# Attention's probabilities normalised inside the product that turns them, dense fillers ahead of waits, and a first retention pass in another order

## The chip, the cores and the metric

## The reference, cut to what matters

The program is a two-layer model (gated delta rule, mLSTM, and their MLPs) followed by a third layer that mixes retention and attention. The change touches waits around mLSTM and around the third layer's context norm, and the two mixers of the third layer:

```
def _dense_attention(q, k, v):                 # 8 query heads, 2 key heads, 512 queries, 768 keys
    s = jnp.einsum('bqkgd,bskd->bkgqs', q, k).astype(jnp.float32) * ATT_SCALE
    p = jax.nn.softmax(s, axis=-1).astype(v.dtype)
    return jnp.einsum('bkgqs,bskd->bqkgd', p, v)

# retention, per head, both directions; chunked in the reference
scores = jnp.einsum('bhid,bhjd->bhij', qf, kf) * intra      # intra: decay by distance
o = (jnp.einsum('bhij,bhjv->bhiv', scores, vf)
     + jnp.einsum('bhid,bhdv->bhiv', qf, state) * q_dec)

# mLSTM ends in a norm over each head, the context in one over its rows
hs = rms_norm(hs, w_norm.reshape(MLSTM_HEADS, MLSTM_DV)) * jax.nn.sigmoid(o...)
hc = _modulate(_rmsnorm(xc, norm1_g), csh1, csc1)
```

All is float32, 512 tokens plus 16 meta tokens.

## The kernel before, in words

Five engines run hand-ordered instruction streams that meet only in semaphores: `S("name")` is a count that one engine adds to and another waits for. There is no scheduler; the order of the code is the order of each engine. Most of the time is PE's: weights are split into a high and a low part (ACT L322 copies the high part, DVE L329 subtracts for the low part), and every product is three matmuls (L306).

**Attention** (`pe_att`, `act_att`, `dve_att`) works in 32 units of 128 queries of one head against 768 keys. For unit n, PE computes the scores into PSUM (L2775, 128x384 twice), DVE takes the row maximum (L2888) and negates it (L2891), ACT computes the exponentials into `a_p` with their row sum (L2827), DVE takes the inverse of the sum (L2895) and multiplies `a_p` (128x768) by it (L2897), PE turns the six 128x128 tiles of `a_p` (L2783), and ACT copies the turned tiles to SBUF (L2848). PE's order per unit is: scores of unit n+2, turning of unit n, and, in three of eight units, a third of the product with the values of the head pair before (L2793). DVE's order is: maximum of unit n+1, then inverse and scaling of unit n. The turned tiles have one place in PSUM (banks 4 and 5), so the turning of unit n waits for the copy of unit n-1. Among the first units stand the norm sums and factors of retention (L2658, L2677, L2711), which share PE and DVE.

**Retention** (`pe_ret`, `act_ret`, `dve_ret`, `pool_ret`) works in two passes of two heads. In each, DVE computes the exponents of the decay table `r_tt` (L2574, L2576) and the decayed context keys (L2582, L2583), ACT the exponentials for the queries (L2553) and the table (L2556), then copies the turned values `r_vT` (L2559); PE waits for `r_vT` and the context keys before the state product (L2633), and for DVE's decayed scores before the next scores (L2607). ACT's and DVE's passes are loops with registers for the pass. Ahead of the first pass ACT splits a block of weights (L322).

**Norms and waits.** `pe_norm` sums squares by a product with ones (L357), and after the inverse root comes back spreads it over rows (L366). It is called for the context (turn 5) between two blocks of the third layer's input product. `pe_mls_gates` turns the gates of mLSTM (L1853, L1854) once DVE has done its part (L1843). At the end of mLSTM PE sums squares of the last chunk in two halves (L1869), turns the statistics (L1937), and spreads the factors of the 8 heads (L1944), from which DVE forms the input of the output product tile by tile (L2101, L2105).

Of the kernel before, what the change touches and what calls it, by code (L numbers as in the profile page):

```python
# [14 lines left out]
P = 128  # L15
# [104 lines left out]
def build_program(nc, A, out):  # L120
    with ExitStack() as ctx:
# [248 lines left out]
        def pe_norm(pe, turn, pieces, sq=n_sq, to=6):  # L370

            pe_norm_sums(pe, turn, pieces, sq, bank=4)
            pe_norm_rows(pe, turn, pieces, to)
# [1475 lines left out]
        def pe_mls_gates(pe):  # L1849
            pe.wait_ge(S("gates_a"), GDN_A + 9)  # L1850
# [331 lines left out]
        a_pT = [at(f"a_pT{y}", [P, KEYS // P, SEQ], SB_G + 4 * 2 * T * 2 + RH * SEQ * 4 + y * KEYS // P * SEQ * 4) for y in range(2)]  # L2182
        a_pT2 = aa_r.take("a_pT2", [P, KEYS // P, SEQ])
# [172 lines left out]
        def pe_b2_in(pe):  # L2356
# [12 lines left out]
            pe_norm(pe, 5, CTXP, sq=ctx_sq, to=5)  # L2369
# [177 lines left out]
        def act_ret(act):  # L2547
            act.sem_inc(S("r_out"), 2)
            with act.Fori(0, RH // 2) as i:
                for x in range(2):  # L2550
                    act.wait_ge(S("r_o"), i * 2 + (x + 1))
                    for d in range(2):
                        act.activation(r_qd[x][d][:, :], b_pos[:, d, :], ACT.Exp, scale=b_lg[:, bass.ds(i * 2 + (RH * d + x), 1)])\  # L2553
                            .then_inc(S("r_qe"), 1)
                    act.wait_ge(S("r_t"), i * 2 + (x + 1))
                    act.activation(r_tt[x][:, :], r_tt[x][:, :], ACT.Exp).then_inc(S("r_te"), 1)  # L2556
                for x in range(2):
                    act.wait_ge(S("v_turned"), i * 2 + (MLS_HALVES + x + 1))
                    act.activation(r_vT[x][:, :, :], ps[:, 4 * x, :].rearrange("p (a t) -> p a t", a=4), ACT.Copy).then_inc(S("v_copied"), 1)  # L2559
                for x in range(2):  # L2560
                    act.wait_ge(S("r_sd"), i * 2 + (x + 1))
                    act.activation(r_S[x][:, :, :], ps[:, 4 * x, 0:2 * P].rearrange("p (a t) -> p a t", a=2), ACT.Copy).then_inc(S("r_S"), 1)
                for x in range(2):
                    fixed_wait(act)
                    act.wait_ge(S("r_o"), i * 2 + (x + 3))
                    act.activation(b_q[:, bass.ds(i * 2 + x, 1), :].rearrange("p a t -> p (a t)"), ps[:, 4 * x + 1, :], ACT.Copy)\
                        .then_inc(S("r_out"), 1)

        def dve_ret(dve):
            with dve.Fori(0, RH // 2) as i:  # L2570
                for x in range(2):
                    lg = [b_lg[:, bass.ds(i * 2 + (RH * d + x), 1)] for d in range(2)]
# [193 lines left out]
        def pe_att(pe):  # L2766
# [463 lines left out]
```

## Time and profile before

| what | value |
|---|---|
| median of 3 runs | 2556.2 us |
| the profiled execution's own time | 2550.86 us |
| its span, first to last instruction | 2549.0 us |
| PE busy | 2453.0 us (96%) |
| DVE, ACT, POOL busy | 56%, 33%, 10% |
| mean granted PE clock | 0.978 |
| the chain that ended last | PE 87%, DVE 7%, ACT 3%, issue 2% |

The chain is followed back from the last instruction to what released it each time; an engine's share in it is time that sets the end. The profiled execution lasted 5.3 us less than the median. Spans are counted from the first instruction.

### The profile page before, as it was taken

How to read it: one execution, taken by the hardware profiler on the slowest of the kernel's cores; microseconds unless marked ns; L12 is line 12 of the kernel's file. 1: busy time of each engine (PE TensorE's matmuls, PEld its weight loads, DVE VectorE, ACT ScalarE, POOL GpSimd, SP SyncE). 2: the span in 40 equal slices, each digit the busy share in tenths (PEclk: the TensorE clock that was granted, in tenths of full speed). 3: DMA queues.
4: the chain of work that ended last, by engine and by line, in shares of the span. 5: the costliest groups of instructions: out<-in, count | busy, mean ns of one | idle time of the engine just before them, and what ended most of it. 6: DMA issues, size and time to landing. Idle time of an engine off the chain costs nothing.

```text
span 2549.0 us, 41060 instructions
## 1 busy us (share of the span) xinstructions
PE 2453.0 (96%) x17237; PEld 2229.6 (87%) x17237; DVE 1415.8 (56%) x1954; ACT 837.5 (33%) x1196; POOL 261.3 (10%) x203
## 2 busy tenths in 40 slices
PE   7999999999999999999998999999999899999998
PEld 7999999998999999999987788888997446998996
DVE  5677656654553443543566666667466464544443
ACT  5433444444321221322323322224323353322332
POOL 2000222323100000100021000002012101000001
PEclk9999999989999999999998999999999899999999
DMA  3222533335222222222101444543311001222221
GB/s 137 83 84 72 129 84 90 87 60 196 83 84 100 83 92 89 94 89 83 66 1 70 154 156 165 182 155 140 108 58 43 17 1 50 83 86 96 99 83 66
DMA packets 93885, 235.70 MB, mean 92 GB/s; under 512 B 60074, under 2 KB 61700, under 8 KB 69556
## 3 DMA queue, kind: packets, MB, share of 16 engines
q1 hardware_dynamic: 88208, 201.40, 23.8%
q10 hardware_dynamic: 5540, 32.30, 3.5%
q8 instruction: 107, 1.75, 0.3%
q14 instruction: 30, 0.25, 0.0%
HBM read 222.00 MB, written 11.67 MB: 92 GB/s over the span
## 4 chain that ended last, share of the span: by engine, by line
PE 87%; DVE 7%; ACT 3%; issue 2%; DMA 1%; POOL 0%; ACTq 0%; DVEq 0%; POOLq 0%; SPq 0%
PE ps L306 68%; PE ps L1128 1%; PE ps L1142 1%; PE ps L2775 1%; PE ps L1118 1%; PE ps L310 1%; PE ps L2793 1%; PE ps L2783 1%; DVE c_DA L2028 1%; PE ps L1154 1%; PE ps L1155 1%; ACT whi L322 1%; PE ps L1160 1%; DVE g_tmp L1342 1%; PE ps L1076 1%
## 5 line engine op out<-in xcount | busy, mean ns | idle before, releaser
L306 PE MATMUL ps<-xa_hi,whi 128*128 128x264 f32 (+2 forms) x2944 | 654.2, 296 | 24.3 <-DVE wlo L329 13.1
L306 PE MATMUL ps<-xa_lo,whi 128*128 128x264 f32 (+2 forms) x2944 | 649.8, 295 | 0.0
L306 PE MATMUL ps<-xa_hi,wlo 128*128 128x264 f32 (+2 forms) x2944 | 649.2, 295 | 0.0
L306 PEld LDWEIGHTS ps<-xa_hi,whi 128*128 128x128 f32 x2944 | 468.7, 190 | 42.1 <-DVE wlo L329 15.1
L322 ACT ACTIVATE whi<-raw 128x2048 fp32r<-128x2048 f32 x161 | 307.4, 1909 | 559.0 <-PE ps L306 546.7
L306 PEld LDWEIGHTS ps<-xa_lo,whi 128*128 128x128 f32 x2944 | 467.8, 190 | 11.1
L306 PEld LDWEIGHTS ps<-xa_hi,wlo 128*128 128x128 f32 x2944 | 467.3, 190 | 10.8
L329 DVE TENSOR_TENSOR wlo<-raw,whi 128x2048 fp32r<-128x2048 f32 x161 | 369.5, 2295 | 189.0 <-ACT whi L322 186.3
L306 PE MATMUL ps<-xb_lo,whi 128*128 128x264 f32 (+1 forms) x1280 | 384.4, 341 | 0.0
L306 PE MATMUL ps<-xb_hi,whi 128*128 128x264 f32 (+1 forms) x1280 | 382.5, 339 | 1.8 <-DVEq L248 1.5
L306 PE MATMUL ps<-xb_hi,wlo 128*128 128x264 f32 (+1 forms) x1280 | 382.6, 340 | 0.0
L306 PEld LDWEIGHTS ps<-xb_hi,whi 128*128 128x128 f32 x1280 | 220.2, 188 | 32.5 <-ACTq L248 2.4
L306 PEld LDWEIGHTS ps<-xb_lo,whi 128*128 128x128 f32 x1280 | 219.7, 188 | 27.9
L306 PEld LDWEIGHTS ps<-xb_hi,wlo 128*128 128x128 f32 x1280 | 220.0, 189 | 27.3
L381 POOL TENSOR_TENSOR n_sq<-n_sq 128x512 f32<-128x512 f32 (+1 forms) x42 | 76.0, 1810 | 1252.4 <-ACT n_sq L391 1250.3
L690 DVE TENSOR_TENSOR h<-ps,h 128x528 f32<-128x528 f32 (+1 forms) x88 | 61.2, 697 | 176.6 <-PE ps L306 175.4
L620 ACT ACTIVATE xb_hi<-m_y 128x528 fp32r<-128x528 f32 (+1 forms) x64 | 40.9, 639 | 280.0 <-DVE m_y L667 280.0
L692 DVE SCALAR_TENSOR_TENSOR h<-ps,b_mod,h 128x512 f32<-128x512 f32 x40 | 30.0, 749 | 113.1 <-PE ps L306 113.1
L865 DVE SCALAR_TENSOR_TENSOR conv_acc<-conv_in,par,conv_acc 128x528 f32<-128x528 f32 x96 | 73.8, 769 | 7.3 <-DVE conv_acc L862 0.2
L664 DVE SCALAR_TENSOR_TENSOR m_act<-ps,rstd 128x528 f32<-128x528 f32 (+1 forms) x64 | 44.5, 695 | 50.5 <-PE ps L306 48.7
L670 DVE TENSOR_TENSOR xb_lo<-m_y,xb_hi 128x528 fp32r<-128x528 f32 (+1 forms) x64 | 44.8, 700 | 45.1 <-ACT xb_hi L620 45.1
L614 ACT ACTIVATE m_y<-m_act 128x512 f32<-128x512 f32 x32 | 23.2, 724 | 115.9 <-DVE m_act L652 115.9
(423 smaller groups left out, 2820.4 us busy)
## 6 DMA issues: line engine op xcount, KB each, us to landing
raw<-weights SPq DMA_DIRECT2D x161, 1024.0 KB, 4.8
mod_w<-weights_mod ACTq DMA_DIRECT2D x24, 1024.0 KB, 4.7
g_EC<-scr_g SPq DMA_DIRECT2D x10, 424.0 KB, 5.2
scr_z<-z_st SPq DMA_DIRECT2D x16, 264.0 KB, 4.6
g_D<-scr_g SPq DMA_DIRECT2D x10, 371.0 KB, 5.2
scr_a<-g_AT SPq DMA_DIRECT2D x10, 318.0 KB
h<-x_in ACTq DMA_DIRECT2D x4, 528.0 KB, 9.5
z_b<-scr_z SPq DMA_DIRECT2D x1, 2112.0 KB
```

Of the source, the lines that this page charges most:

```text
L306: mm = pe.matmul(ps[:, at_ + step * c + bank, 0:tn], w[:, hb.slot, k, c * P:(c + 1) * P], x[:, k, t0:t0 + tn], start=(k == 0 and n == 0), ...
L310: mm = pe.matmul(ps[:, 6 + c, 0:en], w[:, hb.slot, k, c * P:(c + 1) * P], (elo if n == 1 else ehi)[:, k, 0:en], start=(k == 0 and n == 0), ...
L322: act.activation(whi[:, hb.slot], raw[:, hb.raw_slot], ACT.Copy).then_inc(S("w_hi"), 1)
L329: dve.tensor_tensor(wlo[:, hb.slot], raw[:, hb.raw_slot], whi[:, hb.slot].bitcast(F32), ALU.subtract).then_inc(S("w_lo"), 1)
L381: pool.tensor_tensor(flat(sq[:, 0], pieces), flat(sq[:, 0], pieces), flat(sq[:, k], pieces), ALU.add)\
L620: act.activation(flat(xb_hi[:, t], pieces), flat(m_y[:, c], pieces), ACT.Copy).then_inc(S("two_hi"), 1)
L664: dve.scalar_tensor_tensor(cols(m_act[:, c], pieces), pair(c, pieces), 0.0, cols(rstd, pieces), ALU.max, ALU.mult)\
L670: dve.tensor_tensor(flat(xb_lo[:, t], pieces), flat(m_y[:, c], pieces), flat(xb_hi[:, t], pieces).bitcast(F32), ALU.subtract).then_inc(S(" ...
L690: ins = dve.tensor_tensor(x, pair(c, pieces), x, ALU.add)
L692: ins = dve.scalar_tensor_tensor(x, pair(c, pieces), scale(2 * j + c), x, ALU.mult, ALU.add)
L865: ins = dve.scalar_tensor_tensor(conv_acc[:, c, :], x, w, conv_acc[:, c, :], ALU.mult, ALU.add)
L1076: mm = pe.matmul(ps[0:CH, 4 * x + 3, q * P:(q + 1) * P], qkv[:, 8 + 2 * g + q // 2, c], g_S[:, 4 * g + q, :], start=True, stop=True)
```

## The change: what it does

Four edits.

1. In attention, DVE no longer scales the 128x768 probabilities. It scales the 128x128 identity to a diagonal `a_dg` of the inverse sums, and PE multiplies each tile of `a_p` with it, where it turned the tile with `transpose` before.
2. A new helper `pe_keep` issues n float32 matmuls of ones with ones (128x128) into a bank whose contents are dead. 12 go between the context norm's sums and rows, 14 ahead of the gates' wait, 6 and 11 ahead of the two waits of mLSTM's last sums, 5 and 5 ahead of the two waits behind them. A wait for `c_kw` guards the bank.
3. ACT's and DVE's passes over retention are written out without registers. In the first pass ACT copies the turned values before the exponentials, and DVE forms the context keys before the table's exponents. The second pass keeps its order.
4. ACT's split of weights moves from ahead of the first retention pass to behind its state copies.

```diff
+        def pe_keep(pe, n, bank):
+            for _ in range(n):
+                pe.matmul(ps[:, bank, 0:P], ones[:, :], ones[:, :], start=True, stop=True)
...
             pe_norm_sums(pe, turn, pieces, sq, bank=4)
+            pe_keep(pe, keep, to)
             pe_norm_rows(pe, turn, pieces, to)
...
         def pe_mls_gates(pe):
+            pe_keep(pe, 14, 4)
             pe.wait_ge(S("gates_a"), GDN_A + 9)
...
-            def sums(i):
+            def sums(i, keep=(0, 0)):
                 for x in range(2):
+                    pe_keep(pe, keep[x], 1)
                     pe.wait_ge(S("c_sq"), i * 2 + x + 1)
...
-            sums(NCH - 1).then_inc(S("head_sums"), 8)
+            pe.wait_ge(S("c_kw"), 2 * NCH)
+            sums(NCH - 1, (6, 11)).then_inc(S("head_sums"), 8)
 
         def pe_mls_rows(pe):
+            pe_keep(pe, 5, 1)
             pe.wait_ge(S("head_inv"), 6)
...
+            pe_keep(pe, 5, 1)
             pe.wait_ge(S("head_lo"), 3)
...
+        a_dg = [aa_r.take(f"a_dg{c}", [P, P]) for c in range(2)]
...
-            pe_norm(pe, 5, CTXP, sq=ctx_sq, to=5)
+            pe_norm(pe, 5, CTXP, sq=ctx_sq, to=5, keep=12)
...
         def act_ret(act):
...
+            for i in range(RH // 2):
+                for part in (values, decays) if i == 0 else (decays, values):
+                    part(i)
...
+                if i == 0:
+                    act_split(act, HalfBlock(HB_B2_OUT + 1))
...
         def dve_ret(dve):
...
+            for i in range(RH // 2):
+                for part in (context, tables) if i == 0 else (tables, context):
+                    part(i)
...
-                    mm = pe.transpose(ps[:, 4 + t // 3, (t % 3) * P:(t % 3 + 1) * P], a_p[n % 2][:, t * P:(t + 1) * P], ident[:, :])
+                    mm = pe.matmul(ps[:, 4 + t // 3, (t % 3) * P:(t % 3 + 1) * P], a_p[n % 2][:, t * P:(t + 1) * P], a_dg[n % 2][:, :],
+                                   start=True, stop=True)
...
-                    dve.tensor_scalar(a_p[c][:, :], a_p[c][:, :], a_inv[c][:, 0:1], None, ALU.mult).then_inc(S("at_n"), 1)
+                    dve.tensor_scalar(a_dg[c][:, :], ident[:, :], a_inv[c][:, 0:1], None, ALU.mult).then_inc(S("at_n"), 1)
...
-                lambda: (act_split(act, HalfBlock(HB_B2_OUT + 1)), act_ret(act)),
+                lambda: act_ret(act),
```

The order on ACT at the first retention pass, before: `whi` is the weight split, `r_qd` and `r_tt` the exponentials, `r_vT` the turned values, `r_S` the states. The loop begins at L2549, and `r_vT` stands behind its four `r_qd` and two `r_tt`.

```order
L2477 ACTIVATE b_dec<-b_dec 128x16
L322 ACTIVATE whi<-raw 128x2048
L2549 UNCONDITIONAL_BRANCH
L2549 ISA
L2553 ISA
L2553 ACTIVATE r_qd_178<-b_pos,b_lg 128x512
```

And in the change, the same place on ACT:

```order
L2489 ACTIVATE b_dec<-b_dec 128x16
L2574 ACTIVATE r_vT_187<-ps 128x512
L2574 ACTIVATE r_vT_188<-ps 128x512
L2567 ACTIVATE r_qd_178<-b_pos,b_lg 128x512
L2567 ACTIVATE r_qd_179<-b_pos,b_lg 128x512
L2569 ACTIVATE r_tt_185<-r_tt_185 128x896
L2567 ACTIVATE r_qd_180<-b_pos,b_lg 128x512
L2567 ACTIVATE r_qd_181<-b_pos,b_lg 128x512
L2569 ACTIVATE r_tt_186<-r_tt_186 128x896
L2581 ACTIVATE r_S_193<-ps 128x256
L2581 ACTIVATE r_S_194<-ps 128x256
L322 ACTIVATE whi<-raw 128x2048
```

The two value copies now come first, and the split last of the group.

The end of mLSTM on PE before: `c_sq` are the squares, `head_stat` the statistics, `mh_hi` and `mh_lo` the factors.

```order
L1921 MATMUL ps<-c_W_133,c_VA_137 128x106
L1869 MATMUL ps<-ones,c_sq 106x64 x8
L1937 MATMUL ps<-ident,head_stat 8x106 x5
L1944 MATMUL ps<-mh_hi,head_one 128x512
L1944 MATMUL ps<-mh_lo,head_one 128x512
```

And in the change, with the fillers (L373):

```order
L1929 MATMUL ps<-c_W_133,c_VA_137 128x106
L373 MATMUL ps<-ones 128x128 x6
L1877 MATMUL ps<-ones,c_sq 106x64 x4
L373 MATMUL ps<-ones 128x128 x11
L1877 MATMUL ps<-ones,c_sq 106x64 x4
L373 MATMUL ps<-ones 128x128 x5
L1947 MATMUL ps<-ident,head_stat 8x106 x5
L373 MATMUL ps<-ones 128x128 x5
L1955 MATMUL ps<-mh_hi,head_one 128x512
```

27 fillers stand between products that stood next to each other.

The beginning of attention on PE before: `a_kd` and `a_qst` are the scores, `ident` and `a_p` the turning, `rn_sq` retention's norm sums.

```order
L2775 MATMUL ps<-a_kd,a_qst_206 128x384 x2
L2783 MATMUL ps<-ident,a_p_214 128x128 x6
L2775 MATMUL ps<-a_kd,a_qst_207 128x384 x2
L2783 MATMUL ps<-ident,a_p_213 128x128 x6
L2677 MATMUL ps<-ones,rn_sq 128x64 x16
```

And in the change:

```order
L2801 MATMUL ps<-a_kd,a_qst_206 128x384 x2
L2809 MATMUL ps<-a_dg_226,a_p_214 128x128 x6
L2801 MATMUL ps<-a_kd,a_qst_207 128x384 x2
L2809 MATMUL ps<-a_dg_225,a_p_213 128x128 x6
L2703 MATMUL ps<-ones,rn_sq 128x64 x16
```

Nothing moves here; the moving operand of the six products is now the diagonal. These rows count a float32 product once, where the trace shows two matmuls for it: the scores stand as x2 a unit here and as x128 over 32 units in the trace.

## Rows read from the trace of the kernel before

**Rows 1.** The page: busy time, share, instructions.
```profile
PE 2453.0 (96%) x17237; PEld 2229.6 (87%) x17237; DVE 1415.8 (56%) x1954; ACT 837.5 (33%) x1196; POOL 261.3 (10%) x203
```
**Rows 2.** Windows: stretch, length, busy of PE, PEld, DVE, ACT, POOL, PEclk, DMA.
```profile
1175.80:1179.20 3.40, 3.40 (x16) 3.36 (x16) 0.58 (x2) 0.00 (x0) 0.00 (x0) 0.50 0.85 294
1346.40:1363.40 17.00, 13.18 (x37) 9.64 (x38) 10.21 (x18) 7.79 (x14) 1.98 (x1) 0.50 0.00 1
1783.40:1790.10 6.70, 3.08 (x14) 3.08 (x15) 4.27 (x8) 1.50 (x4) 0.00 (x0) 0.50 0.40 126
1954.00:1957.30 3.30, 3.30 (x16) 3.30 (x17) 2.17 (x4) 0.53 (x2) 2.14 (x2) 0.50 0.02 5
2022.40:2035.80 13.40, 11.16 (x27) 6.17 (x28) 7.04 (x15) 5.58 (x9) 0.00 (x0) 0.50 0.00 0
2059.90:2063.20 3.30, 3.30 (x11) 2.24 (x10) 2.33 (x8) 1.49 (x4) 0.00 (x0) 0.50 0.02 5
2111.10:2117.80 6.70, 4.72 (x17) 2.22 (x17) 0.78 (x2) 1.83 (x4) 0.00 (x0) 0.50 0.01 2
```
**Rows 3.** Chain of waits, the context norm: start, length, piece.
```profile
1787.02 1.22 PE ps L366 x4
```
**Rows 4.** Chain of waits, the end of mLSTM.
```profile
1347.42 1.71 PE ps L1869 x8
...
1349.91 1.06 PE ps L1937 x5
...
1352.96 7.19 PE ps L1944 x16
```
**Rows 5.** Timeline, DVE, end of mLSTM's output tiles: start, length, instruction.
```profile
1354.29 1.47 DVE L2101 TENSOR_TENSOR mh_y<-ml,ps 128x512 f32<-128x512 f32 x2 [1.39 <-PE ps L1944]
...
1364.51 1.63 DVE L2105 SCALAR_TENSOR_TENSOR xb_lo<-mh_y,par,xb_hi 128x512 fp32r<-128x512 f32 x2
```
**Rows 6.** Chain of waits, retention: state product and what follows, both passes.
```profile
1953.92 3.65 PE ps L2633 x16
1957.58 3.43 PE ps L2607 x8
...
1977.55 1.78 PE ps L2633 x16
```
**Rows 7.** Timeline, retention's first pass on ACT and DVE.
```profile
1947.15 1.91 ACT L322 ACTIVATE whi<-raw 128x2048 fp32r<-128x2048 f32 x1 [0.27 <-issue]
...
1951.14 0.75 DVE L2582 TENSOR_TENSOR r_ck<-ps,b_dec 128x256 f32<-128x256 f32 x2
...
1953.10 1.06 ACT L2559 ACTIVATE r_vT<-ps 128x512 f32<-128x512 f32 x2
...
1953.70 2.47 DVE L2591 TENSOR_TENSOR r_w<-ps,r_tt 128x512 f32<-128x512 f32 x4
```
**Rows 8.** Attention by form, 1994 to 2122: count, busy us, mean ns, idle before.
```profile
L2783 PE MATMUL ps<-ident,a_p 128*128 128x128 f32 x192 | 30.4, 300 | 16.5 <-DVE a_p L2897 15.5 <-ACT a_pT L2848 1.0
...
L2897 DVE TENSOR_SCALAR a_p<-a_p,a_inv 128x768 f32<-128x768 f32 x32 | 20.5, 639 | 1.1
...
L2891 DVE TENSOR_SCALAR a_nm<-a_mx 128x1 f32<-128x1 f32 x32 | 4.9, 154 | 1.1
```
**Rows 9.** DVE's lines by form, the whole span: the nearest tensor_scalar.
```profile
L455 DVE TENSOR_SCALAR n_y<-n_y,b_modc 128x256 f32<-128x256 f32 x8 | 2.8, 354 | 0.3
```
**Rows 10.** Chain of waits, 1994.3 to 2123.3: shares by line, then three pieces.
```profile
by line: PE ps L2775 22.9%; PE ps L2793 18.2%; PE ps L2783 16.9%; DVE a_mx L2888 8.1%; DVE a_p L2897 5.9%; issue 4.1%; PE ps L2711 2.8%; PE ps L2677 2.7%; PE ps L2658 2.7%; ACT a_p L2827 2.3%; DVE xb_lo L2860 2.1%; ACT xb_hi L2832 1.6%; DVE
...
2045.36 1.87 PE ps L2793 x8
2047.23 1.49 PE ps L2775 x4
2048.72 0.66 PE ps L2783 x6
```
**Rows 11.** Line L2783: what PE's idle time ahead of it ended with.
```profile
  DVE a_p L2897: 44.3, 32
```

More of the change, by code:

```diff
@@ L368, in pe_norm_rows, with pe_norm @@
             mm.then_inc(S("norm_all"), 1)
-        def pe_norm(pe, turn, pieces, sq=n_sq, to=6):
+        def pe_keep(pe, n, bank):
+            for _ in range(n):
+                pe.matmul(ps[:, bank, 0:P], ones[:, :], ones[:, :], start=True, stop=True)
+        def pe_norm(pe, turn, pieces, sq=n_sq, to=6, keep=0):
             pe_norm_sums(pe, turn, pieces, sq, bank=4)
+            pe_keep(pe, keep, to)
             pe_norm_rows(pe, turn, pieces, to)
@@ L2548, in act_ret, with decays @@
             act.sem_inc(S("r_out"), 2)
-            with act.Fori(0, RH // 2) as i:
+            def decays(i):
                 for x in range(2):
@@ L2552, in act_ret, with values @@
                     for d in range(2):
-                        act.activation(r_qd[x][d][:, :], b_pos[:, d, :], ACT.Exp, scale=b_lg[:, bass.ds(i * 2 + (RH * d + x), 1)])\
-                            .then_inc(S("r_qe"), 1)
+                        n = RH * d + 2 * i + x
+                        act.activation(r_qd[x][d][:, :], b_pos[:, d, :], ACT.Exp, scale=b_lg[:, n:n + 1]).then_inc(S("r_qe"), 1)
                     act.wait_ge(S("r_t"), i * 2 + (x + 1))
                     act.activation(r_tt[x][:, :], r_tt[x][:, :], ACT.Exp).then_inc(S("r_te"), 1)
+            def values(i):
                 for x in range(2):
@@ L2562, in act_ret, with tables @@
                     act.activation(r_S[x][:, :, :], ps[:, 4 * x, 0:2 * P].rearrange("p (a t) -> p a t", a=2), ACT.Copy).then_inc(S("r_S"), 1)
+                if i == 0:
+                    act_split(act, HalfBlock(HB_B2_OUT + 1))
                 for x in range(2):
-                    fixed_wait(act)
                     act.wait_ge(S("r_o"), i * 2 + (x + 3))
-                    act.activation(b_q[:, bass.ds(i * 2 + x, 1), :].rearrange("p a t -> p (a t)"), ps[:, 4 * x + 1, :], ACT.Copy)\
-                        .then_inc(S("r_out"), 1)
+                    act.activation(b_q[:, 2 * i + x, :], ps[:, 4 * x + 1, :], ACT.Copy).then_inc(S("r_out"), 1)
         def dve_ret(dve):
-            with dve.Fori(0, RH // 2) as i:
+            def tables(i):
                 for x in range(2):
-                    lg = [b_lg[:, bass.ds(i * 2 + (RH * d + x), 1)] for d in range(2)]
+                    lg = [b_lg[:, RH * d + 2 * i + x:RH * d + 2 * i + x + 1] for d in range(2)]
                     dve.wait_ge(S("r_o"), i * 2 + (x + 1))
@@ L2576, in dve_ret, with context @@
                     dve.scalar_tensor_tensor(r_tt[x][:, :], b_tau[:, 1, :], lg[1], r_tt[x][:, :], ALU.mult, ALU.add).then_inc(S("r_t"), 1)
+            def context(i):
                 for x in range(2):
@@ L2580, in dve_ret @@
                     for d in range(2):
-                        w = b_dec[:, d, bass.ds(i * 2 + x, 1), :].rearrange("p a l -> p (a l)")[:, :, None].to_broadcast([P, 2, P])
+                        w = b_dec[:, d, 2 * i + x, :][:, :, None].to_broadcast([P, 2, P])
                         dve.tensor_tensor(r_ck[x][:, d], c[:, 0], w, ALU.mult)
                     dve.tensor_copy(r_cv[x][:, :, :], c[:, 1]).then_inc(S("r_c"), 1)
+            for i in range(RH // 2):
+                for part in (context, tables) if i == 0 else (tables, context):
+                    part(i)
+                for x in range(2):
                     dve.wait_ge(S("r_te"), i * 2 + (x + 1))
```

## The prediction

> **What bounds the kernel now.** I read the page's busy times first, then the granted clock, then the chain of waits at each place that the change touches. PE is busy 96% of the span [rows 1], so a saving counts only where PE waits, or where its clock is at the lower level. The windows show where it is: seven stretches at 0.50, that is 1.2 GHz, all behind a place where PE stood idle or did little [rows 2]. In such a stretch PE's work takes twice its time. The first four lie where fillers or the retention edit go, the last three in attention. In attention PE's idle time ahead of the turning, 44.3 us over 32 units, ended with DVE's scaling [rows 11]. That looks like the bound, but the chain says otherwise: the scaling has 5.9% of 129.0 us, 7.6 us, the turning itself 16.9%, 21.8 us, and scores and value products 41% [rows 10]. Where a unit has a value product in front, PE goes from one to the next without waiting: 1.87, 1.49 and 0.66 us [rows 10].
>
> **The product with the diagonal.** A turned tile costs 0.66 / 6 = 0.11 us on PE at full clock [rows 10]. A 128x128 float32 product stands in the trace too: retention's state product has 8 of them, as 16 matmuls in 1.78 us, so 0.222 us each; at the lower clock the same took 3.65 us, 0.456 each [rows 6]. The turning is 192 matmuls for 192 tiles [rows 8], one each, where the product needs two. Six tiles so cost 1.33 in place of 0.66 us: +0.67 a unit, and twice that at 1.2 GHz. The ends are 0 (the product runs like the turning) and +2.1 (all at the lower clock: 6 x 0.456 - 0.66); I take +0.67, the row of the same shape.
>
> The Trainium skill speaks against this edit. "Perfetto Trace Analysis", section "Transposes", says that a logical transpose should be issued as a transpose and not as a standard matmul, since transposes skip the arithmetic; and "TensorE: Matmul & The Clock Gate", section "Terms", calls the transpose mode 4 times as fast for FP32. By that figure a tile would cost an estimated 0.44 us; the rows of this case say twice, not four times, and the measurement of the same shape decides for the sum.
>
> DVE's scaling takes 0.62 to 0.64 us for 768 columns, and 0.154 for one [rows 8]; for 256 it takes 0.354 [rows 9]. For 128 I take 0.25, between those last two, which are the ends. The saving is 0.38 us a unit (0.28 to 0.48).
>
> Which unit pays and which saves is read off the chain. The turning has 25 pieces in it, the scaling 12, one of these only 0.04 long. So +0.67 x 25 = +16.8 us and -0.38 x 11 = -4.2. Around 2084 to 2091 the chain runs over DVE alone and a unit lasts 2.0 to 2.4 us; with the product PE needs 1.29 + 1.33 = 2.62 for scores and product, so PE takes over there: +1.2 over three or four units. Against that stands the clock. The stretch at 2059.9 follows 2.1 us of idle PE; the longer products in front of it and the shorter scaling behind leave about 1 us, so I expect it to stay at full clock: 3.3 / 2 = -1.6. The last stretch, 6.7 us with 4.7 of work in it, goes the same way, for the three last turnings come closer together: -1.9 of a possible 2.4. The long one, 13.4 us, begins behind retention's square roots, where PE waits 4.6 us in any case; it falls again, but dense products may end it a step earlier: -1.0 net of what the product costs twice in it. Attention together: 16.8 - 4.2 + 1.2 - 1.6 - 1.9 - 1.0 = **+9.3 us**. If the clock gives nothing back it is +13.8.
>
> **The fillers.** Each is a 128x128 float32 product, 0.222 us at full clock, 0.456 at the lower [rows 6].
> - Gates: 14 make 3.1 us in an idle time of 4.6 that ends with DVE's part at 1175.3, so nothing is late. PE then worked 3.4 us at 0.50 [rows 2]; if the clock stays up, half goes: -1.7. If it falls all the same, 0.
> - Context norm: 12 begin at 1783.1, and the statistics are back at 1787.0 [rows 3]. At full clock they last 2.7 us. But the lower clock began at 1783.4 [rows 2], ahead of them, for the sums before them have one column each; then they last up to 5.4 us and end at up to 1788.5, late by 1.5. They must raise the clock again in that time to pay. PE's work there at 0.50, from 1787.0 to 1790.1, is 3.1 us, half of it 1.5. I take -1.2; the ends are -1.5 and +0.8.
> - End of mLSTM: 6 make 1.3 us in 1.8, 11 make 2.4 in 3.1, so neither is late. The second sums then take 0.88 in place of 1.71, the turning about half of 1.06 [rows 4]; the 5 fillers ahead of it, 1.1 us, end 0.3 us behind DVE's statistics. So the spreading of factors starts 1.0 us earlier, and its first result, at full clock, another 0.5. From there DVE sets the pace, 1.46 us a tile, to the last low part at 1366.1 [rows 5], and PE's tile waits for that: it shifts by 1.5, and PE's slack of 0.5 before it goes too. The factors have 8 rows only and keep the clock low as they did [rows 2], but PE is not late through that. -1.8; the ends are -0.8 and -2.3. The added wait for `c_kw` is met long before: DVE wrote it ahead of the last chunk's products. Behind it stands nothing but the fillers and the sums.
>
> Fillers: -1.7 - 1.2 - 1.8 = **-4.7 us**.
>
> **Retention's first pass.** Before, the state product waits for the value copies, which stand behind a 1.91 us split and all exponentials: 1953.1 [rows 7]. Now the copies begin at 1947.1 and end at 1948.2; DVE's keys, 1.0 us a head [rows 7], end at 1949.3; PE is free from the scores at 1949.7 and does the state product there, 4.2 us earlier. What is late next is DVE's decayed scores, which began at 1953.70 [rows 7]. DVE now has keys, then tables (1.9 a head, to 1953.2), then waits for ACT's exponential of the second table, about 1954.5, and starts at 1954.8, 1.1 later than before. PE's next scores need the first of them, at 1955.5; before, they began at 1957.58 [rows 6], because the state product ran at 1.2 GHz. So 2.1 us are won if these run at full clock. But the idle time only moves, 1951.5 to 1955.5, and the scores inherit the lower clock [rows 2]: I take half, **-1.1 us**; the ends are -2.1 and +0.8 (low twice as long). The second pass keeps its order, and PE is busy through it. The split of weights ends by 1957.3 and is first needed after attention. SP's load behind it waits for DVE's half, which does not move.
>
> **The sum.** +9.3 - 4.7 - 1.1 = +3.5 us. The profiled execution gave 2550.86 us, 5.3 under the median; I take the difference as the same for both kernels, so 2554.4 on its scale and 2556.2 + 3.5 = **2559.7 us** as a median.
>
> **The rivals.**
> - *The wait was the bound (faster).* Mechanism: the product fills idle time of PE, and the shorter scaling is what the next unit sees. For it: 44.3 us of idle time that end with the scaling, over all 32 units [rows 11]. Then only the 10 units behind value products pay 0.67, and 20 save 0.38: +6.7 - 7.6, the clock -2, the other edits -5.8: 2547.5. Against it: 25 turnings are in the chain, and each starts only when the scaling is done, so its own length is never hidden. Chance 0.20.
> - *The clock gives nothing back (slower).* Place: the stretch from 2022.4 and the context norm. Mechanism: attention's products run in low stretches and pay 1.34, the fillers ahead of the norm come late. Attention +13.8, fillers and retention -2.8 together: 2567. It decides once two of the three stretches in attention stay. For it: in the long one PE was busy 11.2 of 13.4 us and the clock did not rise [rows 2]; the spreading products there have 4 rows. Chance 0.30.
> - *The product costs four times a turning.* On PE, 0.33 more a tile: +2.0 in each of 25 units, and the rest as in the sum: 16.8 becomes 50, so 2593. The 1.78 us for 16 matmuls speak against it [rows 6]. This is the skill's figure from "Terms". Chance 0.03.
> - *The product costs what the turning did* (the change adds no PE work): 2559.7 - 16.8 - 1.2 + 2 (less of the clock comes back) = 2543.7. Against it: x192 for 192 tiles here, x16 for 8 products there. Chance 0.07.
>
> **How the numbers follow.** The forecast has 0.40, and its own range is 2556 to 2564. A measurement tells about 0.2% from no change, 5.1 us: faster is under 2551.1, slower over 2561.3. Faster: most of the first rival (0.16) and the last (0.07), 0.23. Slower: 0.24 of the second, 0.03 of the third, 0.08 of the forecast: 0.35. The same: the rest, 0.42. The range runs from the first rival's upper part to the second's price, 2549 to 2567; it leaves out about 0.2.
>
> **What would show it.** The product as x384 matmuls and about 1.33 us for a unit's twelve; 0.25 us for DVE's scaling; periods of about 4.7 us where value products stand (4.0 before) and 2.6 elsewhere; attention about 138 us long in place of 129; a clock near 1 at the gates, at the context norm from 1787 on, around 1347, and at 2060. I am wrong if the product takes another multiple of the turning, if attention gets shorter, or if the stretches at 0.50 stand where they stood.

## The result and the profile after

The changed kernel takes 2567.71 us (median of 5 runs, 2565.24 to 2568.93) against 2555.89 us of the kernel before on the same chip (5 runs, 2551.69 to 2556.23): ratio 1.0048, 95% interval 1.0037 to 1.0059, or 11.8 us slower. The forecast was 3.5 us slower, inside the bound of 0.2%; the result lies beyond that bound and 0.7 us above the upper end of the range, 2567. The profiled execution has a span of 2565.9 us. Its busy times, to be read beside [rows 1]:

```profile
PE 2481.8 (97%) x17535; PEld 2263.0 (88%) x17535; DVE 1410.4 (55%) x1954; ACT 837.2 (33%) x1196; POOL 260.9 (10%) x203
```

PE has 298 instructions more: 192 for the products, 106 for 53 fillers of two each. It is busy 28.8 us longer, and the clock of the span rose from 0.978 to 0.982 at the same time.

To find the place I took the lengths of stages from both traces, from one named instruction to the next. The part ahead of mLSTM's gates, which the change touches only by the 14 fillers at its end, was 3.5 us longer in this execution and varied from 1172.5 to 1182.4 over all profiles taken, with fillers and without; stage lengths are free of that. They are not free of chance: a stage ran shorter or longer between profiles of the same instructions, by up to 2 us, with the length of its stretches at the lower clock.

| stage (us) | before | after | difference | forecast |
|---|---|---|---|---|
| gates' turning to first row product | 74.9 | 73.8 | -1.1 | -1.7 |
| last mLSTM product to context sums | 440.7 | 440.4 | -0.3 | -1.8 |
| context sums to first `b_g` | 150.8 | 149.4 | -1.4 | -1.2 |
| retention's first turning to attention's first scores | 49.9 | 53.1 | **+3.2** | -1.1 |
| attention's first scores to its last value product | 127.0 | 140.0 | **+13.0** | +9.3 |
| behind attention | 427.7 | 427.7 | 0.0 | 0 |

The five changed stages add up to +13.4; 91.1 and 11.5 us of the stages between them did not move. Retention went the other way, attention cost more than was counted, and the fillers gave 2.8 of 4.7.

The windows of the profile after answer to [rows 2] (columns as there; the seventh number is the granted clock):

```profile
1178.90:1182.30 3.40, 3.40 (x29) 3.30 (x30) 0.58 (x2) 0.00 (x0) 0.00 (x0) 1.00 0.65 229
1346.40:1356.80 10.40, 9.02 (x71) 8.13 (x70) 5.46 (x9) 4.08 (x9) 1.98 (x1) 1.00 0.00 1
1356.80:1367.00 10.20, 9.50 (x21) 6.11 (x20) 9.45 (x14) 4.82 (x7) 0.00 (x0) 0.50 0.10 14
1783.40:1790.10 6.70, 4.74 (x40) 4.58 (x41) 3.04 (x5) 2.72 (x3) 0.87 (x2) 1.00 0.14 21
...
1957.00:1965.00 8.00, 6.29 (x8) 2.71 (x9) 5.52 (x8) 1.82 (x2) 0.90 (x1) 0.57 0.00 1
2029.40:2039.40 10.00, 8.65 (x28) 6.52 (x29) 3.35 (x9) 3.23 (x6) 0.00 (x0) 0.50 0.00 0
2059.90:2063.20 3.30, 3.30 (x19) 1.94 (x16) 0.73 (x1) 1.42 (x4) 1.50 (x2) 1.00 0.00 0
```

The clock stays up at the gates and at the context norm, as forecast. The end of mLSTM lies 2.4 us later in this execution. The low stretch there is shorter, 10.2 us in place of 17.0, but it comes later: full to 1356.8 where it had fallen at 1346.4, then 0.50 until 1367.0 where it had ended at 1363.4. In attention the stretches at 2059.9 and 2111 are gone, and the long one lasts 10 us in place of 13.4. In retention there is a longer one.

Attention's chain of waits in the profile after, by line, and three pieces of it (start, length, piece), against [rows 10]:

```profile
by line: PE ps L2809 31.4%; PE ps L2801 21.0%; PE ps L2820 15.5%; DVE a_mx L2915 5.6%; issue 3.3%; DVE a_dg L2924 2.8%; PE ps L2703 2.5%; PE ps L2684 2.5%; PE ps L2737 2.3%; ACT a_p L2854 2.1%; ACT a_pT L2875 1.8%; DVE xb_lo L2887 1.5%; DVE
...
2054.38 1.87 PE ps L2820 x8
2056.25 1.49 PE ps L2801 x4
2057.74 1.34 PE ps L2809 x12
```

L2801 holds the scores, L2809 the product with the diagonal, L2820 the value products, L2924 the diagonal. A unit's product has 12 matmuls in 1.34 us where the turning had 6 in 0.66, and a unit with value products lasts 1.87 + 1.49 + 1.34 = 4.70 us: the price by instruction was right. Summed over its pieces, the product has 44.0 us of the chain in 29 pieces, the turning had 21.8 in 25: +22.2. The scaling went from 7.6 us in 12 pieces to 3.9 in 9, DVE's maxima from 10.5 in 12 to 7.9 in 9. PE's idle time ahead of the line, against [rows 11], and the forms against [rows 8]:

```profile
  DVE a_dg L2924: 29.6, 20
  issue: 5.2, 12
```

```profile
L2809 PE MATMUL ps<-a_dg,a_p 128*128 128x128 f32 x384 | 51.4, 286 | 13.7 <-DVE a_dg L2924 11.7 <-ACT a_pT L2875 2.0
...
L2924 DVE TENSOR_SCALAR a_dg<-ident,a_inv 128x128 f32<-128x128 f32 x32 | 10.4, 324 | 1.1
```

In 12 of 32 units PE does not wait for the diagonal any more. The diagonal takes 0.324 us in the mean (0.25 forecast); the median is 0.286, and the longest of the 32 took 1.03.

Retention's first pass in the timeline after (start, length, instruction, idle time before it), against [rows 6, 7]:

```profile
1949.74 0.67 DVE L2593 TENSOR_SCALAR r_tt<-b_tau,b_lg 128x896 f32<-128x896 f32 x1
...
1950.32 1.95 PE L2659 MATMUL ps<-r_cv,r_ck 128*128 128x128 f32 x16
...
1950.44 2.25 DVE L2595 SCALAR_TENSOR_TENSOR r_tt<-b_tau,b_lg,r_tt 128x896 f32<-128x896 f32 x1
1950.49 3.34 POOL L2557 TENSOR_TENSOR r_qd<-r_qd,b_q 128x512 f32<-128x512 f32 x2 [27.24 <-ACT r_qd L2567]
1952.62 1.69 DVE L2593 TENSOR_SCALAR r_tt<-b_tau,b_lg 128x896 f32<-128x896 f32 x1
...
1954.35 1.15 DVE L2595 SCALAR_TENSOR_TENSOR r_tt<-b_tau,b_lg,r_tt 128x896 f32<-128x896 f32 x1
1955.17 2.73 POOL L2557 TENSOR_TENSOR r_qd<-r_qd,b_q 128x512 f32<-128x512 f32 x2 [1.35 <-ACT r_qd L2567]
1955.42 2.63 DVE L2611 TENSOR_TENSOR r_tt<-r_tt,ident 128x128 f32<-128x128 f32 x2
...
1957.97 2.47 DVE L2617 TENSOR_TENSOR r_w<-ps,r_tt 128x512 f32<-128x512 f32 x4
...
1958.71 6.48 PE L2633 MATMUL ps<-b_q,b_kv 128*128 128x512 f32 x8 [6.44 <-DVE r_w L2617]
```

The state product (L2659) is early and at full clock, as forecast. But of DVE's four table steps the two that ran while GpSimd's products (L2557) were under way, to 1953.83, took 2.25 and 1.69 us; the first, with GpSimd idle, and the last, which GpSimd met only in its last 0.33 us, took 0.67 and 1.15. The two additions of L2611, again beside GpSimd, took 2.63. So the decayed scores began at 1957.97, PE stood idle 6.4 us, and its scores then ran at the lower clock, 6.48 us in place of 3.43.

### The profile page after: what moved, and what is told of

Read it like the earlier page. It is cut to its first block, busy times and chain, and to the rows that moved or that the text cites. A ratio compares the mean times of both kernels' runs of the same rounds, so it can differ in the third digit from the quotient of the medians.

```text
span 2565.9 us, 41587 instructions
## 1 busy us (share of the span) xinstructions
PE 2481.8 (97%) x17535; PEld 2263.0 (88%) x17535; DVE 1410.4 (55%) x1954; ACT 837.2 (33%) x1196; POOL 260.9 (10%) x203
## 4 chain that ended last, share of the span: by engine, by line
PE 87%; DVE 7%; ACT 3%; issue 2%; DMA 1%; POOL 0%; ACTq 0%; DVEq 0%; POOLq 0%; SPq 0%
PE ps L306 68%; PE ps L2809 2%; PE ps L1134 1%; PE ps L1148 1%; PE ps L2801 1%; PE ps L310 1%; PE ps L1124 1%; PE ps L2820 1%; DVE c_DA L2039 1%; PE ps L1160 1%; PE ps L1161 1%; ACT whi L322 1%; DVE g_tmp L1348 1%; PE ps L1166 1%; PE ps L1082 1%
## 5 line engine op out<-in xcount | busy, mean ns | idle before, releaser
L306 PE MATMUL ps<-xa_hi,whi 128*128 128x264 f32 (+2 forms) x2944 | 653.8, 296 | 24.2 <-DVE wlo L329 12.8
L306 PE MATMUL ps<-xa_lo,whi 128*128 128x264 f32 (+2 forms) x2944 | 649.1, 295 | 0.0
L306 PE MATMUL ps<-xa_hi,wlo 128*128 128x264 f32 (+2 forms) x2944 | 648.4, 295 | 0.0
L306 PEld LDWEIGHTS ps<-xa_hi,whi 128*128 128x128 f32 x2944 | 467.8, 190 | 41.9 <-DVE wlo L329 14.8
L306 PEld LDWEIGHTS ps<-xa_lo,whi 128*128 128x128 f32 x2944 | 467.1, 189 | 11.0
L306 PEld LDWEIGHTS ps<-xa_hi,wlo 128*128 128x128 f32 x2944 | 466.4, 190 | 10.9
L306 PE MATMUL ps<-xb_lo,whi 128*128 128x264 f32 (+1 forms) x1280 | 384.9, 341 | 0.0
L306 PE MATMUL ps<-xb_hi,whi 128*128 128x264 f32 (+1 forms) x1280 | 383.0, 340 | 1.8 <-DVEq L248 1.5
L306 PE MATMUL ps<-xb_hi,wlo 128*128 128x264 f32 (+1 forms) x1280 | 383.1, 340 | 0.0
L306 PEld LDWEIGHTS ps<-xb_hi,whi 128*128 128x128 f32 x1280 | 220.5, 188 | 32.9 <-ACTq L248 2.4
L306 PEld LDWEIGHTS ps<-xb_lo,whi 128*128 128x128 f32 x1280 | 220.1, 188 | 27.8
L306 PEld LDWEIGHTS ps<-xb_hi,wlo 128*128 128x128 f32 x1280 | 220.3, 189 | 27.5
L871 DVE SCALAR_TENSOR_TENSOR conv_acc<-conv_in,par,conv_acc 128x528 f32<-128x528 f32 x96 | 73.8, 769 | 7.4 <-DVE conv_acc L868 0.2
L2809 PEld LDWEIGHTS ps<-a_dg,a_p 128*128 128x128 f32 x384 | 49.0, 199 | 25.7 <-DVE a_dg L2924 17.9
```

What stands on the lines that cost most here:

```text
L306: mm = pe.matmul(ps[:, at_ + step * c + bank, 0:tn], w[:, hb.slot, k, c * P:(c + 1) * P], x[:, k, t0:t0 + tn], start=(k == 0 and n == 0), ...
L871: ins = dve.scalar_tensor_tensor(conv_acc[:, c, :], x, w, conv_acc[:, c, :], ALU.mult, ALU.add)
L2809: mm = pe.matmul(ps[:, 4 + t // 3, (t % 3) * P:(t % 3 + 1) * P], a_p[n % 2][:, t * P:(t + 1) * P], a_dg[n % 2][:, :], start=True, stop=True)
```

## The experiments

All ratios are against the kernel before on the same chip, with 95% intervals.

**The change taken apart.** `e1_turned` is the changed kernel with the old attention:

```
-  mm = pe.matmul(..., a_p[...], a_dg[n % 2][:, :], start=True, stop=True)
+  mm = pe.transpose(..., a_p[...], ident[:, :])
-  dve.tensor_scalar(a_dg[c][:, :], ident[:, :], a_inv[c][:, 0:1], None, ALU.mult)
+  dve.tensor_scalar(a_p[c][:, :], a_p[c][:, :], a_inv[c][:, 0:1], None, ALU.mult)
```

> The changed kernel with attention as before: DVE scales the 128x768 probabilities, PE turns them; fillers and the new first retention pass stay. Theory A (the product costs PE 0.67 us more in every unit and the wait it shortens gives 0.32 back in few of them): attention, from its first scores to its last value product, goes from 140 back to 127 us, and the time falls by about 13 us from the changed kernel, to some 2555 us, the level of before. Theory B (the product is nearly free and the loss lies in retention and the fillers): less than 5 us come back, 2563 or more.

Measured: 2554.86 us (12 runs), 0.9995 [0.9985, 1.0004]. Attention 126.4 us, retention 53.2. That is the level of the kernel before, as expected. Fillers and retention together are worth nothing that can be told from zero, and the net loss is attention's. `e11b_att_only` is the other half, the same edit the other way on the kernel before:

> The kernel before with the product by the diagonal alone (fillers and retention as before). Theory (attention is a stage of its own): attention 138.5 to 140 us in place of 127.0, so +11.5 to +13: 2567.5 to 2569 us. Rival (the product's price and the scaling's saving add, +15.8 and -5.1 as measured apart): attention 137.7, 2566.6 us. If part of attention's cost came from where retention leaves the clock, it is under 137.5.

Measured: 2569.21 us (5 runs), 1.0057 [1.0042, 1.0071], attention 140.3. Attention is a stage of its own: its cost is there without the other edits. Over the six profiles with the product by the diagonal it has 138.3 to 140.3 us, over the five with the old attention 126.4 to 127.5, so its cost is read to about 1 us. `e2_ret_back` puts the old retention into the changed kernel (the two loops `for i in range(RH // 2)` and the place of the weight split as before):

> The changed kernel with retention as before: loops with registers, the split of weights first, exponentials and tables first. Theory A (the new order brings DVE's decay tables beside GpSimd's product and makes the decayed scores late): from the first turning of retention to attention's first scores it takes 49.9 us again in place of 53.1; 3 us less than the changed kernel, about 2564.5. Theory B (retention's 3 us in the one profile are chance): within 1 us of the changed kernel, 2567 to 2568.

Measured: 2565.97 us (10 runs), 1.0035 [1.0024, 1.0045]. Retention is back at 50.0, 3.1 us shorter, as expected. The median fell only 1.7 where 3 was expected; the profiled execution was 2.4 us longer behind attention, and two of the ten runs took 2557.9 where the others took 2563.7 to 2568.6. Neither was followed up. Two stages that this edit does not touch differ as well: attention has 138.3 in place of 140.0, and the end of mLSTM 438.9 in place of 440.4. In both the stretch at the lower clock was shorter, 3.4 us in place of 10.0 and 6.8 in place of 10.2. `e10b_fillers_only` has the fillers alone on the kernel before:

> The kernel before with the fillers alone. Theory: gates -1.1, context norm -1.4, end of mLSTM -0.3 (what the second sums win is lost again at the lower clock), together -2.8: 2553.1 us, retention 49.9 and attention 127.0. Rival: what a filler wins is given back later by the clock: within 0.5 us of the kernel before, 2555.4 to 2555.9. By my forecast it would be -4.7, 2551.2.

Measured: 2551.38 us (11 runs), 0.9986 [0.9977, 0.9995], 3.0 us faster than before on that chip, by the same stages as in the changed kernel (73.8, 440.4, 149.4). `e3_no_fillers` is the changed kernel without them (`for _ in range(0)` in `pe_keep`):

> The changed kernel without its fillers. Theory A (fillers give 1.2 us at the gates, 1.4 at the context norm and only 0.3 at the end of mLSTM): 2.9 us slower than the changed kernel, about 2570.5, with the clock at 0.50 behind the gates and behind the norm again. Theory B (they give what was forecast, 4.7): 2572.5. Theory C (nothing): 2567.7.

Measured: 2570.0 us (5 runs), 1.0057 [1.0044, 1.0070], 2.3 over the changed kernel, with intervals that overlap: gates 76.7, context norm's stage 151.0. By stages the fillers hold; the median alone would not tell. Over all profiles the gates' stage has 73.8 or 73.9 with full fillers and 74.9 to 76.7 without, so the 1.1 us is the least that they give there. Retention, which this edit does not touch, has 51.9 here in place of 53.1.

**What in attention costs.** `e5_product_scaled` adds the product to the kernel before and keeps the scaling, so the product is with the identity:

```
-  mm = pe.transpose(..., a_p[n % 2][:, t * P:(t + 1) * P], ident[:, :])
+  mm = pe.matmul(..., a_p[n % 2][:, t * P:(t + 1) * P], ident[:, :], start=True, stop=True)
```

> The kernel before with one edit: the six tiles of a unit are multiplied with the identity in a float32 product, where they were turned; DVE scales the probabilities as before. Theory A (the product's own length sets the loss): +0.67 us in nearly all 32 units, twice where the clock is low, so +19 to +22 us on before, 2576. Theory B (PE's waits for DVE hide it): under +8. The difference of this run to the changed kernel's attention (+13) is what DVE's shorter scaling gives back.

Measured: 2569.8 us (6 runs), 1.0052 [1.0040, 1.0064]; attention 142.8, +15.8, under the 19 to 22 expected. Its chain over attention, by line (L2783 is the product):

```profile
by line: PE ps L2783 30.6%; PE ps L2775 20.6%; PE ps L2794 15.2%; DVE a_mx L2889 5.5%; DVE a_p L2898 4.8%; issue 3.2%; PE ps L2677 2.5%; PE ps L2658 2.4%; PE ps L2711 2.2%; ACT a_p L2828 2.1%; ACT a_pT L2849 1.8%; DVE xb_lo L2861 1.5%; DVE
```

The product has 43.7 us in 29 pieces, as in the changed kernel. Two windows, where the kernel before had its long low stretch and its last one:

```profile
2031.00:2041.10 10.10, 7.58 (x22) 5.19 (x23) 4.85 (x10) 4.06 (x6) 0.00 (x0) 0.50 0.00 0
...
2128.00:2142.40 14.40, 10.57 (x64) 6.49 (x62) 4.26 (x11) 4.90 (x8) 0.00 (x0) 1.00 0.00 1
```

Only the long one is left. Before, PE worked 19.2 us at the lower clock in attention (11.16 + 3.30 + 4.72, [rows 2]), which costs an estimated 9.6 (half of it); here 7.6, which costs 3.8. So the clock gave back about 5.8, and without it the product costs an estimated 15.8 + 5.8 = 21.6 us, as much as 0.67 in each of 32 units. `e4_turn_unscaled` has the turning as before and writes the diagonal in place of the scaling; the probabilities stay unnormalised:

```
-  dve.tensor_scalar(a_p[c][:, :], a_p[c][:, :], a_inv[c][:, 0:1], None, ALU.mult)
+  dve.tensor_scalar(a_dg[c][:, :], ident[:, :], a_inv[c][:, 0:1], None, ALU.mult)
```

> The kernel before with one edit: DVE scales the 128x128 identity, and PE turns the probabilities unscaled, so the output lacks the normalisation. It has the short scaling of the change without its product. Theory A (the scaling is on the chain in 11 of 32 units, 0.32 us each): attention 127.0 us becomes 123.5, the time 3.5 us less than before. Theory B (every one of the 32 waits ends with the scaling): -0.32 x 32, attention 117.

Measured: 2549.44 us (7 runs), 0.9974 [0.9963, 0.9985]; attention 121.9, -5.1 where -3.5 was expected. Its low stretches:

```profile
2026.70:2033.10 6.40, 5.61 (x14) 3.26 (x15) 2.80 (x9) 2.79 (x5) 0.00 (x0) 0.50 0.00 0
2108.40:2118.80 10.40, 8.42 (x27) 3.77 (x27) 0.45 (x2) 2.03 (x4) 0.00 (x0) 0.52 0.01 2
```

PE works 14.0 us at the lower clock, 7.0 lost in place of 9.6, so 2.6 of the 5.1 is the clock and 2.5 the shorter instruction. The stretch at the end stayed with the turning and is gone in the kernels with the product. The two prices together would be +10.7; the stage grew by 13.0 and 13.3 with both edits. With the product there, the short scaling is worth 142.8 - 140.3 = 2.5 us as measured. `e11b_att_only` worked 9.1 us at the lower clock against 7.6, so without the clock it is an estimated 3.2, against the 2.5 here.

**What stretched DVE.** `e6_pool_short` is the changed kernel with GpSimd's products of the first pass cut to one column (the decayed queries of two heads are left out but for it). GpSimd's loop over the passes is written out for it, which the cut below leaves away:

```
+  w = 1 if i == 0 else SEQ
-  pool.tensor_tensor(r_qd[x][d][:, :], r_qd[x][d][:, :], q, ALU.mult)
+  pool.tensor_tensor(r_qd[x][d][:, 0:w], r_qd[x][d][:, 0:w], q[:, 0:w], ALU.mult)
```

> The changed kernel, but GpSimd's products of queries and decays in the first retention pass take one column each in place of 512, so the output of two retention heads is wrong. Theory A (GpSimd's products, which read SBUF at the same time, stretch DVE's table from 1.15 to 2.25 and from 0.67 to 1.69 us): both go back, DVE's first decayed scores come 3 us earlier, and retention takes 49 to 50 us in place of 53.1. Theory B (DVE is stretched by something else in the new order, ACT's copies or PE): the long instructions stay, 53 us.

Measured: 2563.16 us (11 runs), 1.0031 [1.0022, 1.0040]; retention 47.3, 5.8 shorter than in the changed kernel and shorter than the 49 to 50 expected. The timeline on DVE and GpSimd, then two pieces of the chain:

```profile
1952.26 1.17 DVE L2596 SCALAR_TENSOR_TENSOR r_tt<-b_tau,b_lg,r_tt 128x896 f32<-128x896 f32 x1
1952.30 1.18 POOL L2558 TENSOR_TENSOR r_qd<-r_qd,b_q 128x1 f32<-128x1 f32 x2 [27.24 <-ACT r_qd L2568]
1953.36 0.67 DVE L2594 TENSOR_SCALAR r_tt<-b_tau,b_lg 128x896 f32<-128x896 f32 x1
```

```profile
1957.46 3.70 PE ps L2634 x8
1961.16 1.72 PE ps L2669 x4
```

With GpSimd out of the way DVE's steps are back at 1.17 and 0.67. Counted from retention's first turning the scores begin at 10.5 us, where it is 13.6 in the changed kernel, and they take 3.70 us in place of 6.48. It is GpSimd's work beside DVE that stretched the tables, as the theory said. That accounts for 3.1 of the 5.8 us; the rest is the clock, which did not fall here. In the kernel before the same products ran beside DVE's keys and decayed scores, which have one input in PSUM and kept their length (0.75 for two, 2.47 for four, [rows 7]); its GpSimd:

```profile
1950.58 5.56 POOL L2545 TENSOR_TENSOR r_qd<-r_qd,b_q 128x512 f32<-128x512 f32 x4 [28.06 <-ACT r_qd L2553]
```

The Trainium skill, "SBUF — State Buffer", section "Who interferes with whom", states this: an instruction of DVE with two inputs in SBUF, or a `tensor_scalar` in one of its two-port modes, contends with GpSimd for a shared port, and whichever issues first blocks the other. The trace agrees on which forms are hit. On who is first it agrees where the order is clear. In the kernel before and in `e7_dve_order` (below) the last two-input table step began 0.51 and 0.23 us ahead of GpSimd's first product: DVE kept its 1.15 us, and GpSimd's product took 1.78 and 2.05 us where its median is 1.32. In the changed kernel the stretched L2595 began 0.05 us ahead of GpSimd by the records, too close to decide.

`e7_dve_order` keeps the full products and gives DVE the old order, tables first, with ACT's new one:

```
-  for part in (context, tables) if i == 0 else (tables, context):
+  for part in (tables, context):
```

> The changed kernel with DVE's old order in the first retention pass (tables, then context keys); ACT keeps the new one. Theory A (two tables in front run before GpSimd begins, 3.8 us of DVE, then the keys read PSUM): no instruction is stretched, the state product starts about 8 us and the next scores 10 us behind the first turning, retention 47.5 to 48.5 us in place of 53.1 and 49.9 before; about 2563. Theory B (a state product later than in the change keeps the low clock, as before): 50, no better than before.

Measured: 2562.7 us (11 runs), 1.0025 [1.0015, 1.0034]; retention 49.9, no better than before. From its timeline and chain:

```profile
1950.99 1.15 DVE L2595 SCALAR_TENSOR_TENSOR r_tt<-b_tau,b_lg,r_tt 128x896 f32<-128x896 f32 x1
1951.22 5.83 POOL L2557 TENSOR_TENSOR r_qd<-r_qd,b_q 128x512 f32<-128x512 f32 x4 [27.24 <-ACT r_qd L2567]
...
1954.05 1.87 DVE L2611 TENSOR_TENSOR r_tt<-r_tt,ident 128x128 f32<-128x128 f32 x2
```

```profile
1956.58 6.19 PE ps L2633 x8
```

All but the last 0.9 us of the tables is over before GpSimd starts, and no table step is stretched; only the additions of L2611 are. Counted from retention's first turning, the scores begin 2.9 us earlier than in the changed kernel, but inherit the lower clock. I had expected 47.5 to 48.5, with the clock back sooner. `e8_best` puts together the fillers, ACT's new order, DVE's old one, and the old attention.

> Fillers, ACT's new order and DVE's old order in the first retention pass, and attention as before. If the parts add up: fillers -2.9, retention -2 on before: 2551.5, faster than before and than the change.

Measured: 2548.99 us (9 runs), 0.9976 [0.9966, 0.9986], faster than both kernels and 2.5 us below what was expected. Its interval overlaps that of the fillers alone (0.9977 to 0.9995), so that retention's order adds anything to them is not shown. Its profiled execution was the fastest of the nine, 2542.48 us. Retention there, in the same order as `e7_dve_order`, has 47.9:

```profile
1949.35 4.17 PE ps L2633 x8
```

The same order gave 6.19 and 4.17 us for these eight matmuls. The windows from where they begin, of `e7_dve_order` and of `e8_best`:

```profile
1956.50:1959.70 3.20, 3.12 (x4) 1.51 (x5) 2.51 (x5) 1.56 (x1) 0.56 (x1) 0.50 0.03 8
1959.70:1962.80 3.10, 3.10 (x6) 1.25 (x5) 1.38 (x2) 0.00 (x0) 0.00 (x0) 0.69 0.00 0
```

```profile
1949.30:1950.30 1.00, 0.95 (x1) 0.50 (x2) 1.00 (x2) 1.00 (x2) 0.52 (x1) 0.50 0.02 8
1950.30:1953.50 3.20, 3.20 (x9) 1.47 (x8) 2.77 (x5) 1.00 (x1) 0.00 (x0) 0.99 0.00 0
```

The clock was at 0.50 in both when they began; it came back more than 3.2 us later in the one, 1.0 us later in the other. Which of the two an execution gets was not controlled, so 2 us of this stage are not the order's.

**What a filler must be.** `e9b_thin_fillers` is the changed kernel with the old attention and fillers of 8 rows, as many matmuls of as many columns:

```
-  pe.matmul(ps[:, bank, 0:P], ones[:, :], ones[:, :], start=True, stop=True)
+  pe.matmul(ps[:, bank, 0:P], ones[0:8, :], ones[0:8, :], start=True, stop=True)
```

> The changed kernel with the old attention, each filler multiplying 8 rows of ones by 8 rows of ones where it was 128 by 128: the same number of matmuls of 128 columns, the same durations. Theory (the array has to be filled by data, not only by instructions): behind mLSTM's gates and behind the context norm the granted clock is 0.50 as in the kernel before; from the gates' turning to the first row product 75 to 76.7 us in place of 73.8, from the context sums to the first b_g 150.8 to 151 in place of 149.4, about 2558 us as a median. Rival (any run of matmuls does): both stages as in the kernel with full fillers, 73.8 and 149.4, about 2555 us.

Measured: 2561.55 us (9 runs), 1.0028 [1.0018, 1.0037], more than the 2558 expected. Windows behind the gates, at the end of mLSTM and at the context norm, then five fillers (ten matmuls) in its chain and in that of the changed kernel:

```profile
1183.00:1186.30 3.30, 3.30 (x15) 3.25 (x16) 0.58 (x2) 0.00 (x0) 0.00 (x0) 0.50 0.83 303
1353.80:1374.00 20.20, 20.20 (x67) 16.05 (x67) 11.43 (x20) 8.35 (x15) 1.98 (x1) 0.50 0.00 0
1794.00:1800.60 6.60, 6.60 (x31) 6.38 (x31) 4.35 (x8) 0.89 (x4) 0.00 (x0) 0.50 0.48 161
```

```profile
1356.81 2.43 PE ps L373 x10
```

```profile
1350.76 1.17 PE ps L373 x10
```

The clock fell in all three places, though PE had stood idle no longer ahead of them than with full fillers (1.2 us ahead of the gates' turning, against 1.4). At the end of mLSTM it fell at 1353.8, when PE had been busy since 1350.9 and in 22 of these matmuls since 1351.8. The fillers behind, now at twice their length, made the work behind them late: the three stages have 75.4, 443.1 and 151.4 us, against 73.8, 440.3 and 149.4 in `e1_turned`. The rival (any run of matmuls does) falls.

## Why the prediction was wrong

**Retention: the step that failed.** The forecast had DVE's tables "1.9 a head, to 1953.2" and the decayed scores at 1954.8. The order was right, and so were the copies, the keys and the state product. What failed is the length of the tables and of the two additions behind them, taken from a stage in which GpSimd was hardly at work beside them: in the kernel before its products ran from 1950.58, when all but 0.6 us of the tables was done. Moving DVE's keys in front put the tables beside them. Counted from the first turning, PE's scores began 0.4 us later than before where the forecast had them 2.1 earlier, and `e6_pool_short` brings 3.1 us of that start back. The second error is the clock: that the scores would inherit the lower one was forecast and came, but at half of 2.1, 1.0 us, where 6.48 in place of 3.43 is 3.0. The two together are 4.5 us, against the 4.3 by which the stage missed its forecast (+3.2 for -1.1). The forecast's worse end, +0.8, had the low clock in it and no wait for GpSimd.

**Attention: mechanism right, sizes off.** The product was to cost +16.8 on 25 units and +1.2 on the rest, the shorter scaling to save 4.2, the clock to give back 4.5. The runs show, as estimates free of the clock, +21.6 for the product (`e5_product_scaled`) and -3.2 for the scaling with the product there; the clock, with PE's 8.65 us at 0.50 in the changed kernel in place of 19.2, gave 5.3. That makes 13.1 for the 13.0 measured. The largest error is in the product: +18.0 was the charge, 3.6 too little. The units in which the chain of before ran over other engines were left free or nearly so, while the product is paid for as if in all 32; the chain has it in 29 pieces, four more. The count can't be taken from the old chain, for each edit by itself moves it: 29 pieces of product or turning and 9 of scaling stand in the chain of `e5_product_scaled` and in that of `e4_turn_unscaled`, 25 and 12 in the kernel before. The scaling's saving was counted on 11 pieces of the old chain, of which 9 were left. The rival in which the wait was the bound falls with `e5_product_scaled`. The rival with 2567 us came nearest in time, but that is luck: two of the three low stretches in attention went and the clock did give back, so its mechanism is not what happened. The product at four times a turning, or at the same price, falls by the 1.34 us.

**Fillers: two of three right.** Gates -1.1 and norm -1.4 (forecast -1.7 and -1.2), the norm's without the lateness that I feared: the clock did not fall ahead of the fillers in the kernel after, and they were done before the statistics. That is not so in every execution. In the profiles of `e2_ret_back` and `e8_best` the clock fell to 0.50 at these 12 fillers. They took 4.5 and 4.2 us in place of 2.9 and ended 0.5 and 0.2 us behind the statistics; the stage still had only 149.6 and 149.7.

At the end of mLSTM the fillers did what they were to do, up to the first output tile. The step that failed is "from there DVE sets the pace": in the kernel before PE already led there, with 7.19 us of spreading products [rows 4], and in the kernel after the low clock came at 1356.8 and stayed to 1367.0, and the last spreading products, which I had taken as not late, ended the chain:

```profile
1359.02 0.70 DVE mh_y L2112
1359.71 0.04 issue
1359.76 1.22 PE ps L1955 x2
1360.98 11.09 PE ps L306 x35
```

L306 behind them began 1.6 us earlier in its stage than before (1360.98, less the shift of 2.4, against 1360.15), but ran 6.0 us at 0.50, to 1367.0, where it had run 3.3. That takes 1.4 back, and of the forecast's 1.8 us (a shift of 1.5, and part of a slack of 0.5 that it left unworked) 0.3 were left. Six of the seven profiles with full fillers have 440.0 to 440.4 here, against 440.4 to 441.0 without. The seventh, `e2_ret_back`, has 438.9: its low stretch ended earlier, and the whole forecast gain was there. The spreading products ahead have 8 rows, like the fillers of `e9b_thin_fillers` in which the clock fell; that this is the reason here was not tried.

**The sum.** By stages the forecast missed by 4.3 us in retention, 3.7 in attention and 1.9 in the fillers. Measured: fillers -2.8, retention +3.2, attention +13.0, together +13.4 against +11.8 measured between medians; the difference is within the interval of the ratio (9.5 to 15.1 us). `e10b_fillers_only` and `e11b_att_only` give -3.0 and +14.8 directly. Open is what decides when the clock comes back: it is worth about 2 us inside retention's scores, and 1.5 to 2 us at the end of mLSTM and in attention, between executions with the same instructions there.

## What to carry to other kernels

Where PE sets the pace nearly everywhere, folding a scale into a turning trades a DVE instruction that hides for PE time that cannot: price it in every unit, also in those where another engine leads before the change. Before a two-input step of DVE is moved, look at what GpSimd does at the new time, not at the step's length where it stands. Fillers paid here where they were full products and dense work followed, even in the two profiles in which they ended 0.2 and 0.5 us behind the awaited result; where thin work followed, most of the gain was given back in six profiles of seven.

## What the hardware showed that was not expected

- DVE beside GpSimd: steps on 128x896 in SBUF that began during its products went from 1.15 to 2.25 us (two tensor inputs) and from 0.67 to 1.69 (one). Two 128x128 additions took 2.63 us, where one takes 0.28 in `e6_pool_short`. The kernel before had a hint of it, in the spread of the same additions over its two passes (minimum, median, maximum in ns), which a group's mean hides:

```profile
L2585 DVE TENSOR_TENSOR r_tt<-r_tt,ident x4: 358/507/1270, 1952.1 to 1976.3; 128x128 f32<-128x128 f32 x4
```

- Five fillers (ten matmuls) of 8 rows took 2.43 us where five of 128 rows took 1.17: the same columns, but the granted clock had fallen to 0.50 during uninterrupted work on 8 rows.
- With the product with the identity in place of the turning the low stretch at attention's end was gone (`e5_product_scaled`, 1.00 from 2128 to the end), with the turning it stayed (`e4_turn_unscaled`, 0.50 from 2108.4). It is so in all thirteen profiles: gone in the seven with a product, there in the six with the turning. PE was also busier for its longer products, so no run here tells whether it is the kind of instruction or the time.
- DVE's `tensor_scalar` on 128x128 takes 0.286 us (the median of 32, in the changed kernel; 0.287 in `e4_turn_unscaled`), as against 0.354 for twice the columns [rows 9]: I had taken 0.25.
